# A hybrid decoder step on one core: the order of values, turns, exponentials, copies, scaling and sums in each beat of the prompt's attention pairs

## What is computed

```python
def masked_softmax(s, mask):
    s = jnp.where(mask, s.astype(jnp.float32), -1e30)
    p = jax.nn.softmax(s, axis=-1)
    return jnp.where(mask, p, 0.0)
...
    s = jnp.einsum('bnqgjd,bnkgd->bgjnqk', qblk, kb) * NSA_SCALE
    p = masked_softmax(s, mask).astype(qg.dtype)
    o = jnp.einsum('bgjnqk,bnkgd->bnqgjd', p, vb)
...
def mem_attend(q, kv):
    s = jnp.einsum('bthd,bmhd->bhtm', q, kv[:, :, 0]) * MEM_SCALE
    p = jax.nn.softmax(s.astype(jnp.float32), axis=-1).astype(q.dtype)
    return jnp.einsum('bhtm,bmhd->bthd', p, kv[:, :, 1]).reshape(B, T, MEM_Q)
...
    def step(S, xs):
        q_i, k_i, u_i, w_i, a_i, d_i = xs
        v_new = u_i - jnp.einsum('bhcd,bhde->bhce', w_i, S)
        o = jnp.einsum('bhcd,bhde->bhce', q_i * jnp.exp(d_i)[..., None], S) + jnp.einsum('bhij,bhje->bhie', a_i, v_new)
        S = S * jnp.exp(d_i[..., -1])[..., None, None] + jnp.einsum('bhcd,bhce->bhde', k_i * jnp.exp(d_i[..., -1:] - d_i)[..., None], v_new)
        return S, o
```

## Time and profile before

| | us |
|---|---|
| median of 3 runs | 1651.75 |
| lowest and highest | 1646.45 and 1655.67 |
| the profiled execution, its own time | 1652.14 |
| its span in the profile | 1650.4 |
| the stretch of the pairs, first scores to last sum | 569.60 to 817.9 |

### The profile page before, as it was taken

One profiled execution on the slowest core, in us unless ns is written; L12 is line 12 of the kernel. 1 busy time (PEld: TensorE's weight loads), 2 busy tenths in 40 slices (PEclk: granted clock), 3 DMA queues, 4 the chain that ended last, 5 costly groups with the idle time before them and its releaser, 6 DMA issues. The chain is left out here.

```text
span 1650.4 us, 27073 instructions
## 1 busy us (share of the span) xinstructions
PE 1446.0 (88%) x11327; PEld 1314.5 (80%) x11327; DVE 890.2 (54%) x1626; ACT 383.3 (23%) x891; POOL 82.0 (5%) x76
## 2 busy tenths in 40 slices
PE   6999899889968686878766679999989999999998
PEld 5778789789957565656544479899978999999998
DVE  3455256747633565666442355545746746465563
ACT  3543023222232334354422221000003101000000
POOL 0000001100011111111100000000000000000000
PEclk8999999999968697989978889999999999999999
DMA  9132035151321000010167532322340332323221
GB/s 349 65 119 100 10 97 183 59 197 56 118 53 52 0 1 1 1 52 1 39 226 299 201 123 77 116 90 91 102 155 26 103 103 77 103 77 102 89 91 52
DMA packets 115649, 159.03 MB, mean 96 GB/s; under 512 B 6039, under 2 KB 106839, under 8 KB 112778
## 3 DMA queue, kind: packets, MB, share of 16 engines
q1 hardware_dynamic: 111886, 122.76, 22.9%
q0 software_dynamic: 2304, 33.56, 5.1%
q10 hardware_dynamic: 1348, 1.12, 0.2%
HBM read 145.04 MB, written 16.66 MB: 98 GB/s over the span
## 5 line engine op out<-in xcount | busy, mean ns | idle before, releaser
L330 PE MATMUL ps<-uH,wh 128*128 128x260 f32 x576 | 165.8, 288 | 8.7 <-DVE wt L301 8.7
L330 PE MATMUL ps<-hH,wh 128*128 128x260 f32 x512 | 145.7, 285 | 2.6 <-DVE hT L301 2.6
L330 PE MATMUL ps<-mergedH,wh 128*128 128x260 f32 x512 | 145.7, 285 | 0.0
L330 PE MATMUL ps<-hT,wh 128*128 128x260 f32 x512 | 145.4, 284 | 0.0
L330 PE MATMUL ps<-hH,wl 128*128 128x260 f32 x512 | 145.1, 283 | 0.0
L330 PE MATMUL ps<-mergedT,wh 128*128 128x260 f32 x512 | 144.8, 283 | 0.0
L330 PE MATMUL ps<-mergedH,wl 128*128 128x260 f32 x512 | 144.5, 282 | 0.0
L457 PE MATMUL ps<-XT,w 128*128 128x256 f32 (+1 forms) x512 | 126.3, 388 | 6.3 <-DVE XT L520 6.0
L330 PEld LDWEIGHTS ps<-uH,wh 128*128 128x128 f32 x576 | 109.9, 191 | 13.6 <-DVE wt L301 8.9
L330 PE MATMUL ps<-uL,wh 128*128 128x260 f32 x384 | 108.7, 283 | 0.0
L330 PE MATMUL ps<-uH,tw 128*128 128x260 f32 x384 | 108.7, 283 | 0.0
(11 more groups left out here) (530 smaller groups left out, 3430.9 us busy)
## 6 DMA issues: line engine op xcount, KB each, us to landing
wt<-in_w_ff SPq DMA_DIRECT2D x32, 1024.0 KB, 5.3
wt<-in_w_in SPq DMA_DIRECT2D x15, 1024.0 KB, 5.6
tw<-in_w_in SPq DMA_DIRECT2D x12, 1024.0 KB, 5.3
ring<-in_cache_mem_kv SPq DMA_DIRECT2D x4, 2048.0 KB, 11.6
w<-in_cmp_w SPq DMA_DIRECT2D x8, 512.0 KB, 6.1
ring<-in_cache_win_kv SPq DMA_DIRECT2D x2, 2048.0 KB, 8.8
out_s_win<-in_cache_win_kv SPq DMA_DIRECT2D x1, 4088.0 KB
scratch_uhigh<-uH SPq DMA_DIRECT2D x1, 2080.0 KB
```

Of the source, the lines that this page charges most:

```text
L330: ins = pe.matmul(out, lhsT(i, c), rhs(j, c), start=(first and c == 0 and k == 0), stop=(last and c == chunks - 1 and k == 2))
```

## The change

Only the numbers that set the order of the pairs' steps inside a beat are changed, on three engines. On TensorE values go to 0.3 of the beat, ahead of the turns, which go to 0.55 and 0.75. On ScalarE the exponentials go to 0.35, ahead of the copies at 0.6 and 0.8. On VectorE the sums go from 0.8 to 0.45 and the scaling from 0.9 to 0.7. No instruction is added or taken away.

```diff
                     yield beat(u, 0.3)
+                    if u >= 2:
+                        values(u - 2)
+                    yield beat(u, 0.55)
                     if 1 <= u <= NU:
                         turn(u - 1, 0)
-                    yield beat(u, 0.5)
-                    if u >= 2:
-                        values(u - 2)
-                    yield beat(u, 0.6)
+                    yield beat(u, 0.75)
                     if 1 <= u <= NU and rounds_of(u - 1) == 2:
                         turn(u - 1, 1)
...
                     yield beat(u, 0.35)
+                    if u < NU:
+                        exp(u)
+                    yield beat(u, 0.6)
                     if 1 <= u <= NU:
                         keep(u - 1, 0)
-                    yield beat(u, 0.55)
-                    if u < NU:
-                        exp(u)
-                    yield beat(u, 0.65)
+                    yield beat(u, 0.8)
                     if 1 <= u <= NU and rounds_of(u - 1) == 2:
                         keep(u - 1, 1)
...
-                    yield beat(u, 0.8)
+                    yield beat(u, 0.45)
                     if u >= 2:
                         finish(u - 2)
                         dve.wait_ge(o_done, u - 1)
-                    yield beat(u, 0.9)
+                    yield beat(u, 0.7)
                     if u < NU and pairs[u][0] < 2:
                         scale(u)
```

## The result

| | before | with the change |
|---|---|---|
| median, us | 1651.8 (20 runs) | 1658.23 (20 runs) |
| lowest and highest | 1646.45 and 1657.64 | 1650.4 and 1664.7 |
| ratio, 95% interval | 1 | 1.0035 [1.0019, 1.0051] |
| the profiled execution, its time and its span | 1652.14 and 1650.4 | 1659.19 and 1657.4 |

The forecast was 1649 in a range of 1636 to 1664. The time lies in the range and within 0.5% of before, but on the other side: 3 us less were forecast, and the kernel became about 6 us slower, which is clear of the interval.

What follows compares the result with a forecast made beforehand. No engine was full; TensorE was taken as closest to the bound. The terms -3.0 - 6.3 + 1.9 + 1.8 - 0.4 + 3.0 gave -3.0 us against 1652.14, so 1649, range 1636 to 1664.

Steps and rivals of the forecast that it cites:

- tiles 1 and 2: First two query tiles: shorter waits ahead of turns, exponentials and scores; -3.0 us in tile 1, -6.3 in tile 2.
- beats 20 to 30: Two-round pairs: the second round waits for a copy behind the exponentials; 78.0 us walked against 76.05 before, +1.9.
- beats 31 to 38: Later two-round pairs, with the same wait ahead of the second round; 51.65 us walked against 49.87 before, +1.8.
- tail: The last beats, behind the DeltaNet's end, were said to keep their chain; -0.4 us.
- the clock: Tiles 3 and 4: time at TensorE's lower clock level, which the full-speed estimate left out; +3.0 us.
- start and rest of the program: Everything before and behind the stretch of the pairs was said to keep its order; 0 us.
- The calm beats: Beats such as 36, where TensorE is the bound and no order can save anything; 5.75 us forecast there instead of 6.07.
- the walk: Beat-by-beat estimate at full clock: an instruction starts 0.1 us after its engine and inputs are ready; old beat 36: 6.0, trace 6.07.
- Long beats: Two-round beats where the scaling, then the exponentials, held a DeltaNet level up; said to gain, while short ones lose.
- a rival: The faster case, chance 0.25, which added that the scaling's new place may avoid L1784's slowing, 1.70 us against 0.6.
- The slower one: Rival, chance 0.20: the second round of turns bounds 13 beats at 1 us each, with lower clock; +14 us, 1666.
- The faster one: Rival, chance 0.25: waits ahead of turns were the bound and two thirds of 30 us go; stretch 15 us shorter, 1637.

Runs made afterwards that it cites:

- e12: The kernel with the change, with VectorE's scaling at 0.75 of a beat instead of 0.7; 1650.2 us, ratio 1.0002 to the kernel before.
- e10: The kernel with the change, with the old order of all three engines from beat 39 on; 1653.6 us, ratio 1.0013 to the kernel before.
- e5: The kernel with the change, with the old order in the first two query tiles and the new in the last two; 1669.9 us, ratio 1.0122 to before.
- e1: The kernel with the change, with TensorE's old order back (values between the two rounds of turns); 1654.1 us, ratio 1.002 to the kernel before.
- e7: The kernel with the change, with the second round of turns in bank 3 instead of bank 2; 1642.5 us, ratio 0.9952 to before.
- e2: The kernel with the change, with ScalarE's old order back (copies ahead of the exponentials); 1669.4 us, ratio 1.0123 to the kernel before.
- e4: The kernel with the change, with the new order in the first two query tiles and the old in the last two; 1640.0 us, ratio 0.9945 to before.

## Why the prediction went wrong, by its steps

| step | forecast | measured |
|---|---|---|
| tiles 1 and 2 | -9.3 | -8.3 |
| beats 20 to 30 | +1.9 | +5.9 |
| beats 31 to 38 | +1.8 | +7.3 |
| tail | -0.4 | +3.1 |
| the clock | +3.0 | in the rows above |
| start and rest of the program | 0 | -1.0 |
| sum | -3.0 | +7.0 |

**Tiles 1 and 2: right in sum and mechanism, less so in the parts.** Tile 1 gained 5.1 instead of 3.0, tile 2 only 3.1 instead of 6.3. Beat 12 went as walked (2.4 us less, 2.7 forecast). Beat 13 gave 1.2 us of the 2.0 expected, and the giving back in beat 15 came as foreseen: 11.94 us instead of 10.04, where e12, with the scaling behind the products, has 10.10. So beats 12 to 15 gained 1.7 us instead of 3.0, and beats 16 to 19 gained 0.8 instead of 2.2. The wait ahead of the turn in beat 12 was forecast near 3.5 us and is 4.61.

**The calm beats: right.** For thirteen of the nineteen beats from 20 to 38 (20 to 26, 29, 33, 35 to 38; sorted out afterwards, by how close walk and trace are) my walk has 88.3 us and the trace 88.5. Before they took 85.6, so the loss in them was forecast at 2.7 us and was 2.9. The wait that I foresaw, thirteen times 1 to 2 us for L1713, is there fourteen times, up to 5.4 us. The waits for the scaling are gone from these tiles, as forecast, but for the 2.0 us of "issue" ahead of L1634 in beat 27.

**The seam beats: the terms that were mis-sized.** The other six (27, 28, 30, 31, 32 and 34) take 50.6 us where the walk has 41.3 and before had 40.3. "Long beats, where the scaling and then the exponentials held a level up, gain" is the sentence that failed: in beats 27, 28, 32 and 34 the walk gains 3.3 us, and they lost 3.2. Three reasons have a row:

- *A place misread (beat 34).* I let the maximum go ahead of the DeltaNet's updates. In the program they stand ahead of it, and the whole chain shifts behind them:

```profile
766.89 1.13 PE L1621 MATMUL ps<-memhl 64*128 64x512 f32 x4
...
770.04 0.69 DVE L1463 SCALAR_TENSOR_TENSOR g_kb<-ps,g_qe 128x512 f32<-128x512 f32 x1
...
771.23 1.23 DVE L1775 TENSOR_REDUCE nm<-ps 128x2 f32<-128x1024 f32 x1
...
772.49 0.69 ACT L1704 ACTIVATE Pb<-ps,nm 128x512 f32<-128x512 f32 x1 [4.91 <-DVE nm L1775]
...
775.04 1.09 PE L1634 MATMUL ps<-consts,Pb 128*128 128x128 f32 x4 [2.82 <-ACT XT L1713]
...
778.87 1.13 PE L1621 MATMUL ps<-memhl 64*128 64x512 f32 x4
```

  From scores to the second round that is 8.15 us, where the walk's chain allowed 5.6. The beat takes 11.98 us where the walk has 8.9: half of the 3.1 us is the lower clock behind the second round (1.5, above), the rest this place.

- *A slower scaling (beat 27).* The walk gave L1784 its usual 0.6 to 0.75 us. Beside GpSimd's multiplication it took 1.83:

```profile
710.88 0.81 DVE L1782 TENSOR_TENSOR rg<-rg,gate 128x2 f32<-128x2 f32 x1
...
711.72 1.83 DVE L1784 TENSOR_SCALAR Pb<-Pb,rg 128x384 f32<-128x384 f32 x2
711.74 1.26 POOL L1503 TENSOR_TENSOR proj<-proj,g_sq 128x512 f32<-128x512 f32 x1
```

  Before, the scaling took 1.73 us in this beat, so it isn't a new loss but one that the walk had left out. I had hoped in a rival that the new place would avoid it; here it doesn't, since both stand behind the same chunk's end. The Trainium skill (SBUF — State Buffer, "Who interferes with whom") says that VectorE shares one pair of its ports with GpSimd, and that an instruction that takes the pair (a VectorE `tensor_scalar` in a two-port mode can) holds it to its end, while the other engine blocks entirely. Which mode L1784 runs in, the trace doesn't show. By that rule one would expect L1784 to be longer by about one GpSimd instruction, 1.26 us, and the trace agrees: 1.83 is 1.1 more than its usual time.

- *The scaling ahead of the DeltaNet's work (beats 15, 31).* Seen in the prediction for beat 15, and the walk of beat 31 had it (8.0 us, measured 8.7), but as one term among others. e12 shows what the choice is worth: 5.1 us in these two beats, and 5.5 to 8 us of the kernel's time, for 0.05 of a beat. The walk never asked what the beat would be without it.

Some of the 9.3 us is not order but clock: beats 30 and 34 were 2.8 us shorter in e10, with the same instructions there and a higher clock. What else made beat 30 long (5.29 us before, 7.2 in the walk) has no row here.

**The tail: sign wrong.** "The last beats, behind the DeltaNet's end, keep their chain" failed: without the DeltaNet's groups to fill in, the second round, its copy and the values make one chain, 3.1 us longer. e10 shows it, with 2.6 us given back.

**The clock: too small, and its cause open.** I took +3.0 for both tiles from before's share of lower clock. At the two levels of 1.2 and 2.4 GHz a mean of 0.85 over 86.9 us is (1 - 0.85) / 0.5 x 86.9 = 26 us at the lower one; before it was 4 us. TensorE's busy time in the stretch rose from 191.5 to 198.1 us with the same instructions. How much of these 6.6 us lies on the path is not shown; beat 34 alone has 1.5. The obvious reading, that the second round's waits lowered the clock, is not shown either: e5, with the same order in tile 4, has 0.85 as well, but e1, where the waits are as long (30.8 us), has 0.91 there. I had named tiles 3 and 4 becoming shorter, or a clock below 0.85, as signs that the forecast is wrong. Neither came (0.90 and 0.85), so both were set too wide.

**The rivals.** The slower one, "the second round of turns is the bound", is nearest to what happened. Its mechanism is what e7 confirms (17 us in tiles 3 and 4). Its price for these tiles was 13 + 3 + 3 = 19 us and 16.2 were measured; that the two are close is partly luck, since the loss was not 1 us in each of 13 beats but sat mostly in six, and 3.1 us of it in the tail was in no term. It also halved the gain of tiles 1 and 2, which came nearly whole, so its 1666 was too high. The chain that it names, up to a copy behind the exponentials, is what holds TensorE up (e2); that the rounds now stand back to back, which both the prediction and the rival's count of 13 beats go by, is not (e1). The faster one's gain was real as well, but only where there is one round: 7.9 of the 11.6 us of e4's stretch lie in tiles 1 and 2.

## What to carry to other kernels

A change of order should be priced class by class (here: pairs with one round and with two), since a change near zero can be a gain and a loss that a switch by class separates. In an in-order program, what is put first on an engine decides what waits behind it; a resource that two steps share (here one PSUM bank for two rounds) turns that into a wait on another engine. Here taking the sharing away (e7, 1642.5) and switching the order by class (e4, 1640.0) came out alike, and either beat the change and the kernel before. When walking a beat, the calm ones come out right; the error sits where a second program meets it, so there each neighbour on each engine must be looked up, and the walk done with and without each step that could go on either side.

## What the runs showed that I had not expected

- The clock moved by more than the idle time alone accounts for. In the fourth tile its mean fell from 0.97 to 0.85 while TensorE's idle time rose only from 12.4 to 19.8 us, and in the 35.7 us behind the stage, where the kernel is the same, it was 0.69 instead of 0.75. The same beat with the same order ran at 0.86 in one kernel and at 1.00 in another, 1.5 us apart.
- 16 us of useless transposes ahead of the second rounds cost the kernel nothing that can be measured (1654.7 for 1658.2).
- A multiplication of 128x2 elements on VectorE takes 0.16 us alone, and 0.81 and 1.12 us beside a GpSimd multiplication (beats 27 and 12), so even the smallest step behind GpSimd's work is not free.
